# Expert blocks of 112 tokens instead of 128 in a mixture-of-experts layer on one core

## The reference, cut to what matters

```python
def moe_ffn(h, router_w, router_b, w_gu, b_gu, w_down, b_down):
    logits = _f32(xf @ router_w + router_b)
    top_v, top_i = lax.top_k(logits, TOP_K)          # TOP_K = 4 of N_EXPERTS = 32
    gates = jax.nn.softmax(top_v, axis=-1)
...
    def expert_block(args):
        x_blk, e = args
        gu = x_blk @ w_gu[e] + b_gu[e]               # (rows, 1024) @ (1024, 2048)
        gate = jnp.minimum(gu[:, :D_FF], SWIGLU_LIMIT)
        up = jnp.clip(gu[:, D_FF:], -SWIGLU_LIMIT, SWIGLU_LIMIT)
        act = (up + 1.0) * (gate * jax.nn.sigmoid(SWIGLU_ALPHA * gate))
        return act @ w_down[e] + b_down[e]           # (rows, 1024) @ (1024, 1024)
...
    y = jnp.zeros((N, D), h.dtype).at[stok].add(yb[dest] * sg[:, None].astype(h.dtype))
```

## Time and profile before

| | |
|---|---|
| time, median of 3 runs | 1618.28 us (1616.44 to 1618.72) |
| span of the profiled execution | 1615.2 us |
| TensorE busy | 1545.4 us, 96% of the span |
| VectorE busy | 1353.5 us, 84% |
| ScalarE busy | 988.6 us, 61% |
| GpSimd busy | 188.3 us, 12% |
| moved by DMA | 506.83 MB, 314 GB/s on average |

### The profile page before, as it was taken

How to read it: one execution, slowest core, us unless ns; L and a number is a source line. 1 busy time by engine, 2 the same in 40 slices (tenths; PEclk the granted TensorE clock), 3 DMA queues, 4 the chain that set the end, 5 groups by cost and what they waited for, 6 DMA issues and landing times.

```text
span 1615.2 us, 22190 instructions
## 1 busy us (share of the span) xinstructions
PE 1545.4 (96%) x8314; PEld 1169.8 (72%) x8314; DVE 1353.5 (84%) x1059; ACT 988.6 (61%) x798; POOL 188.3 (12%) x210
## 2 busy tenths in 40 slices
PE   3999989998999999999999999999999999999996
PEld 2444358857577787888888888888888888888873
DVE  5557447487878999999999999999999999999987
ACT  4112233343356776777777777777777777777772
POOL 1000111000101200000001000000110000010051
PEclk9999999998899999999999999999999999999998
DMA  9686121215569998999999999999999999999993
GB/s 374 251 342 235 43 92 29 67 57 205 215 251 351 358 384 334 389 387 387 382 387 375 382 396 386 384 389 384 384 378 387 389 385 389 381 390 376 374 380 121
DMA packets 85763, 506.83 MB, mean 314 GB/s; under 512 B 11008, under 2 KB 12336, under 8 KB 33360
## 3 DMA queue, kind: packets, MB, share of 16 engines
q1 hardware_dynamic: 70880, 453.85, 72.1%
q0 software_dynamic: 9104, 34.08, 5.8%
q10 hardware_dynamic: 5728, 18.18, 2.8%
HBM read 477.25 MB, written 28.84 MB: 313 GB/s over the span
## 4 chain that ended last, share of the span: by engine, by line
PE 85%; DVE 9%; DMA 2%; issue 1%; ACT 1%; SPq 0%; POOL 0%; DVEq 0%; POOLq 0%; ACTq 0%
PE ps L2132 62%; PE ps L1219 8%; PE ps L2148 2%; DVE w_lo L1481 2%; PE ps L1296 2%; PE ps L1225 2%; DMA Wt<-in_ada_w 2%; PE ps L2111 2%; PE ps L2121 1%; PE ps L2043 1%; PE ps L1194 1%; PE ps L1167 1%; DMA h_rows<-R 1%; PE ps L2154 1%; PE ps L1186 0%
## 5 line engine op out<-in xcount | busy, mean ns | idle before, releaser
L1481 DVE TENSOR_TENSOR w_lo<-w_raw,w_hi 128x2048 fp32r<-128x2048 f32 x384 | 865.0, 2288 | 72.9 <-ACT w_hi L1475 72.6
L1475 ACT ACTIVATE w_hi<-w_raw 128x2048 fp32r<-128x2048 f32 x384 | 736.6, 1920 | 293.1 <-PE ps L2132 293.1
L2132 PE MATMUL ps<-w_hi,xTh 128*128 128x512 f32 x1024 | 409.1, 399 | 6.5 <-DVE w_lo L1481 5.8
L2132 PE MATMUL ps<-w_lo,xTh 128*128 128x512 f32 x1024 | 402.4, 393 | 0.0
L2132 PE MATMUL ps<-w_hi,xTl 128*128 128x512 f32 x1024 | 276.1, 392 | 0.0
L2132 PEld LDWEIGHTS ps<-w_hi,xTh 128*128 128x128 f32 x1024 | 194.8, 190 | 60.5 <-issue 16.7
L2132 PEld LDWEIGHTS ps<-w_hi,xTl 128*128 128x128 f32 x1024 | 193.8, 189 | 40.6
L2132 PEld LDWEIGHTS ps<-w_lo,xTh 128*128 128x128 f32 x1024 | 194.7, 190 | 38.8
L2132 PE MATMUL ps<-w_hi,aTh 128*128 128x512 f32 x512 | 202.4, 395 | 0.0
L2132 PE MATMUL ps<-w_lo,aTh 128*128 128x512 f32 x512 | 199.4, 389 | 0.0
L2132 PE MATMUL ps<-w_hi,aTl 128*128 128x512 f32 x512 | 157.6, 389 | 0.0
(11 more groups left out here) (404 smaller groups left out, 1407.8 us busy)
## 6 DMA issues: line engine op xcount, KB each, us to landing
w_raw<-in_moe_w_gu SPq DMA_DIRECT2D x256, 1024.0 KB, 6.4
w_raw<-in_moe_w_down SPq DMA_DIRECT2D x128, 1024.0 KB, 7.2
Wt<-in_ada_w SPq DMA_DIRECT2D x19, 1024.0 KB, 10.3
y_rows<-R ACTq DMA_DIRECT2D x30, 512.0 KB, 6.7
Wt<-in_w_in SPq DMA_DIRECT2D x5, 2048.0 KB, 13.6
y_rows<-Wt POOLq DMA_DIRECT2D x1, 8704.0 KB, 40.5
R<-in_ada_w SPq DMA_DIRECT2D x5, 1024.0 KB, 8.1
R<-in_x SPq DMA_DIRECT2D x2, 2048.0 KB, 10.3
```

The source lines that it names most:

```text
L1475: nc.scalar.activation(w_hi[:, at[-1] % HI_SLOTS, :], w_raw[:, at[-1] % RAW_SLOTS, :], ACT.Copy).then_inc(hi_rdy, 1)
L1481: nc.vector.tensor_tensor(w_lo[:, s, :], w_raw[:, s, :], w_hi[:, at[-1] % HI_SLOTS, :].bitcast(F32), ALU.subtract).then_inc(lo_rdy, 1)
L2132: ins = mm(ps[:, bank0 + c, :], x[:, k, :], w[:, 512 * (banks * i + c):512 * (banks * i + c) + 512], start=(first and i == 0 and x is xh a ...
```

## The change

`BLK`, the tokens of a block, goes from 128 to 112. The overflow list has to grow, since more blocks could be needed in the worst case: `MAXOV` is now 2048 // 113 = 18 instead of 15, and `NB` 50 instead of 47. Everything that touches a block's tokens is cut to 112 columns or partitions. Division by 128 was a shift and becomes a sum of comparisons.

```diff
-BLK = 128
-MAXOV = 15
+BLK = 112
+MAXOV = TOPK * S // (BLK + 1)
 NB = E + MAXOV
...
-        slotI = sb("slotI", [P, TT * TOPK], U32)
-        ti = sb("ti", [P, TT * TOPK], U32)
...
-            pool.dma_start(y_d[(E - 2) * BLK:NB * BLK, :].rearrange("(b p) d -> p b d", p=P),
-                           zero_src.unsqueeze(1).to_broadcast([P, MAXOV + 2, D])).then_inc(y_zero, 16)
+            pool.dma_start(y_d[(E - 2) * BLK:NB * BLK, :].rearrange("(b p) d -> p b d", p=BLK),
+                           zero_src[0:BLK].unsqueeze(1).to_broadcast([BLK, MAXOV + 2, D])).then_inc(y_zero, 16)
...
-        xTh, xTl, aTh, aTl = [sb(name, [P, KT, BLK], F32R) for name in ("xTh", "xTl", "aTh", "aTl")]
+        xTh, xTl, aTh, aTl = [sb(name, [P, KT, P], F32R)[:, :, 0:BLK] for name in ("xTh", "xTl", "aTh", "aTl")]
...
-                nc.gpsimd.indirect_dma_start(out=xg[s], out_offset=None, in_=h2_d,
+                nc.gpsimd.indirect_dma_start(out=xg[s][0:BLK], out_offset=None, in_=h2_d,
...
-                s_.activation(dst[:], ps[:, 4:6, :].rearrange("p b (k t) -> p (b k) t", k=4), ACT.Copy
+                s_.activation(dst[:], ps[:, 4:6, :].rearrange("p b (k t) -> p (b k) t", k=4)[:, :, 0:BLK], ACT.Copy
...
-                act.dma_start(y_d[bass.ds(n * BLK, BLK), :], ysb[s]).then_inc(y_out[s], 16)
+                act.dma_start(y_d[bass.ds(n * BLK, BLK), :], ysb[s][0:BLK]).then_inc(y_out[s], 16)
...
-                link(v.tensor_copy(slotI[:, ks], slotf[:, ks]))
-                link(v.tensor_scalar(ti[:, ks], slotI[:, ks], 7, None, ALU.logical_shift_right))
-                link(v.tensor_copy(over[:, ks], ti[:, ks]))
+                link(v.tensor_scalar(over[:, ks], slotf[:, ks], float(BLK), None, ALU.is_ge))
+                for b in range(2, (S - 1) // BLK + 1):
+                    link(v.scalar_tensor_tensor(out=over[:, ks], in0=slotf[:, ks], scalar=float(BLK * b), in1=over[:, ks],
+                                                op0=ALU.is_ge, op1=ALU.add))
...
-            for b in range(2, S // BLK):
+            for b in range(2, (S - 1) // BLK + 1):
                 link(v.scalar_tensor_tensor(out=ovf[:], in0=total_e, scalar=float(BLK * b + 1), in1=ovf[:],
                                             op0=ALU.is_ge, op1=ALU.add))
...
-                v.tensor_tensor(lo_part[:], ps[:, 4:6, :].rearrange("p b (k t) -> p (b k) t", k=4),
+                v.tensor_tensor(lo_part[:], ps[:, 4:6, :].rearrange("p b (k t) -> p (b k) t", k=4)[:, :, 0:BLK],
                                 hi_part[:].bitcast(F32), ALU.subtract).then_inc(lo_sem, 1)
...
-                    ins = nc.tensor.transpose(ps[:, 4 + k // 4, P * (k % 4):P * (k % 4) + P],
-                                              xg[s][:, P * k:P * k + P], ident[:])
+                    ins = nc.tensor.transpose(ps[:, 4 + k // 4, P * (k % 4):P * (k % 4) + BLK],
+                                              xg[s][0:BLK, P * k:P * k + P], ident[0:BLK, 0:BLK])
...
-                        mm(ps[:, 2 * g + c, :], sel[rows, 0:1].to_broadcast([2 * E, P]), bparts[rows, g, :],
+                        mm(ps[0:BLK, 2 * g + c, :], sel[rows, 0:1].to_broadcast([2 * E, BLK]), bparts[rows, g, :],
...
-                                ins = mm(ps[:, bank0 + c, :], x[:, k, :],
+                                ins = mm(ps[0:BLK, bank0 + c, :], x[:, k, :],
```

More of the change, by code:

```diff
@@ L295, in build @@
         pick = Rc(19872, 19872 + TT * TOPK * E).rearrange("p (m e) -> p m e", e=E)
+        cmp = Rc(19872, 19872 + MAXOV * E).rearrange("p (m e) -> p m e", e=E)
         iotaL = Rc(14336, 14336 + BLK)
@@ L1545, in _ @@
             for s in range(2):
-                rows_of(tok[:, s:s + 1], s)
+                rows_of(tok[0:BLK, s:s + 1], s)
             with pool.Fori(1, E // 2) as m:
@@ L1876, in swiglu @@
                 wait_used(dve, gu_end)
-                v.tensor_scalar(two(act_b), ps[:, 2:4, :], 1.0 - LIMIT, 1.0 + LIMIT, ALU.max, ALU.min).then_inc(up_rdy, 1)
+                sig, act_ = sig_b[0:BLK], act_b[0:BLK]
+                v.tensor_scalar(two(act_), ps[0:BLK, 2:4, :], 1.0 - LIMIT, 1.0 + LIMIT, ALU.max, ALU.min).then_inc(up_rdy, 1)
                 dve.wait_ge(sig_rdy, n + 1)
                 dve.wait_ge(up_rdy, n + 1)
-                v.scalar_tensor_tensor(out=act_b, in0=sig_b, scalar=sat[:, 0:1], in1=act_b, op0=ALU.min,
+                v.scalar_tensor_tensor(out=act_, in0=sig, scalar=sat[0:BLK, 0:1], in1=act_, op0=ALU.min,
                                        op1=ALU.mult).then_inc(half_rdy, 1)
                 dve.wait_ge(half_rdy, n + 1)
-                v.scalar_tensor_tensor(out=two(act_b), in0=ps[:, 0:2, :], scalar=LIMIT, in1=two(act_b), op0=ALU.min,
+                v.scalar_tensor_tensor(out=two(act_), in0=ps[0:BLK, 0:2, :], scalar=LIMIT, in1=two(act_), op0=ALU.min,
                                        op1=ALU.mult).then_inc(act_rdy, 1)
@@ L2102, in _ @@
                 for block in ((block_p, block_t) if m >= TOPK else (block_p,)):
-                    ins = mm(ps[:, 6, 0:NB], lane_oh[:, m, :], block[:, m, :], start=(m == 0),
+                    ins = mm(ps[0:BLK, 6, 0:NB], lane_oh[:, m, :], block[:, m, :], start=(m == 0),
                              stop=(m == TT * TOPK - 1 and block is block_t))
@@ L2147, in at_turn @@
                     j, i = k // 2, k % 2
-                    ins = nc.tensor.transpose(ps[:, 4 + k // 4, P * (k % 4):P * (k % 4) + P],
-                                              act_b[:, 2 * P * j + i:2 * P * (j + 1):2], ident[:])
+                    ins = nc.tensor.transpose(ps[:, 4 + k // 4, P * (k % 4):P * (k % 4) + BLK],
+                                              act_b[0:BLK, 2 * P * j + i:2 * P * (j + 1):2], ident[0:BLK, 0:BLK])
                 ins.then_inc(at_mm, 1)
@@ L2188, in tail_turn @@
                     for t in range(TT):
-                        ins = nc.tensor.transpose(ps[:, 4 + i, P * t:P * t + P], tailG[:, TT * i + t, :], ident[:])
+                        ins = nc.tensor.transpose(ps[0:BLK, 4 + i, P * t:P * t + P], tailG[:, TT * i + t, :], ident[:])
                 ins.then_inc(tail_mm, 1)
```

27 lines of the change are left out of this document (13 added, 14 removed).

## The result

| | before | after |
|---|---|---|
| time, median of 6 runs each, side by side | 1617.26 us (1615.31 to 1618.72) | 1621.89 us (1620.71 to 1624.17) |
| span of the profiled execution | 1615.2 us | 1621.0 us |

The ratio is 1.003, 95% interval 1.0019 to 1.004: the change makes the kernel slower by 0.3%. The forecast was 1615.9 us with 1611.0 to 1620.7, so the time moved the other way and lies just outside the range. The two profiled spans differ by 5.9 us and the medians by 4.6: the rest is the spread from run to run.

The account below looks back on a forecast made before the run. The prediction took TensorE's matmul starts to bound the expert loop, with VectorE leading earlier from the routing on. Exposed loads -1.7, routing +0.4 and copies -1.1 gave -2.4 us from 1618.3: 1615.9 us, range 1611.0 to 1620.7.

Parts of the forecast that it names:

- The 4608 products: Experts' float32r matmuls on TensorE: fewer stationary columns leave their start distance unchanged; taken 0, bounds 0 and -2.3 us.
- Exposed loads: Four weight loads an expert that stand alone where the matmul stream breaks get an eighth shorter: -1.7 us.
- Transposes: 16 an expert on TensorE: the 128-column load sets their pace, so taken 0; -6.6 us if the stream did.
- Routing: VectorE's chain to the token list: extra comparison steps and changed one-hot sizes, +0.4 us in sum.
- The bf16 loads: 28 routing matmul loads, now 112 columns, keep their 25 ns pace: taken 0, other end +2.0 us.
- Rival 2: Products' 13.4 ns beyond their stream follow the loaded columns: 7.7 us more gain, 1608.2 us; chance 0.10.
- rival 1: Small bfloat16 routing loads lose their fast pace below 128 columns: +2.0 us, 1617.9 us; chance 0.33.
- Shorter copies: VectorE and ScalarE copies on the chain of waits, outside the TensorE-bound stretch, handle fewer elements: -1.1 us.
- rival 3: TensorE's clock falls once less (-2.8 us, chance 0.07) or once more (+2.8 us, chance 0.06) around the routing and early experts.
- Overflow: Overflow list stays empty, as the fullest expert has 96 tokens, below 112: nothing gained or lost.
- Rival 4: 4-byte loads under 128 columns take a slower way, exposed ones cost +13.3 us: 1630.9 us; chance 0.05.
- rival 5: Overflow list not empty: an entry costs a whole expert's weights, at least 35.4 us, over 1653 us; chance 0.02.

Follow-up runs that it names:

- e4: Kernel before with the experts' products and biases at 96 stationary columns instead of 128; products 230.0 ns apart, its time is not in the text.
- e6: Kernel before with the experts' products and biases at 80 stationary columns instead of 128; 1638 us.
- e8: e7 with blocks of 104 tokens instead of 112; 1615.79 us, ratio 0.9997 to the kernel before.
- e1: Kernel before with only the 4608 products at 112 stationary columns, biases and all else at 128; 1630.05 us, ratio 1.0061.
- e2: Kernel before with 32 bytes of unused memory ahead of the expert buffers, so only addresses move; 1617.9 us, ratio 1.0.
- e3: Kernel after with products, biases and the copies xTh, xTl, aTh, aTl back at 128 columns; 1615.07 us, ratio 0.9987 to the kernel before.
- e7: e3 with the lane one-hots of the bf16 routing matmuls also back at 128 columns; 1616.17 us, ratio 0.998 to the kernel before.
- e10: Kernel before with products and their biases at 112 stationary columns; 1630.73 us, ratio 1.0076.

## Why the prediction was wrong, step by step

- **The 4608 products, taken 0, bounds 0 and -2.3 us: this step failed.** Measured +2.27 ns x 4608 = +10.4 us. The mechanism was named only as what would make the prediction wrong ("a start distance of products that moves by a nanosecond"), and got no chance in the sum. Three things led there. First, the rows were of another kind of matmul. The earlier trace rows have 431 ns with 16 short loads among 48 and 429 without, and distance by distance the trace shows that these 2 ns are not in the short ones: the matmuls with 128 stationary columns start 429 ns apart, those with 8 start 429 ns apart, and a single break of 523 ns where the one follows the other makes the mean. The two halves of the row, first 128 columns, then 8:

```profile
160.72 13.04 PE L1219 MATMUL ps<-R,Wt 128*128 128x512 f32 x30
```

```profile
174.12 7.03 PE L1219 MATMUL ps<-R,Wt 128*8 128x512 f32 x16
```

(13.04 - 0.59)/29 and (7.03 - 0.59)/15 are both 0.429 us. So "120 columns less give 0" was read rightly for float32, which takes 429 ns for 512 columns; it did not carry over to float32r, which takes 227, and no row had a float32r product with fewer columns. Second, 0.32 - 0.094 is 0.226 and not 0.222 us, which leaves about 1 ns to the load and not 4: the lower bound of -2.3 us had no ground. Third, the upper bound was closed at 0 with no row behind it; nothing in the trace excluded a loss. Rival 2, with the sign of a gain, had 0.10, while the same size upward had no rival at all. The rule of the Trainium skill that was set aside (page "TensorE: Matmul & The Clock Gate", section "The mechanism" of Part 3: a load overlaps running matmuls only where the row groups differ) would have given a gain of 61 us, by the estimate of the prediction. The same section also has a load pulled ahead where it targets a background weight buffer, which the prediction left out. The traces disagree with the rule as the prediction used it, here even in sign: in e4 and e6, with a quarter and three eighths fewer columns to load, the products came later.
- **Exposed loads, -1.7 us: half right.** Behind the biases the second product follows the first after 327 ns instead of 338, behind the activations' transposes after 305 instead of 314, behind the gathered rows' after 300 instead of 314: 34 ns an expert, 1.1 us. The changes to and from the biases take 326 and 326 instead of 318 and 315, which gives 20 ns back, and the four biases by themselves, the fourth place counted, take 331 ns instead of 342. That leaves 26 ns an expert, 0.8 us.
- **Transposes, taken 0, bound -6.6 us: mis-sized.** The 8 of the gathered rows went from 109 to 96 ns, 7 distances or 0.090 us an expert, -2.8 us; those of the activations, with their stride of two, from 118.3 to 115.6 ns in the mean, -0.6 us, and the product behind them follows after 55 ns instead of 39, which takes 0.5 back. The router's matmuls were the wrong neighbours: they come at 0.11 us with 32 moving columns, but the transposes, with as many columns to load, came down to 96 and in e8 to 89 ns, so the load does not set a transpose's pace at 109 ns (the transposes' loads also last 140 ns in the trace, the router's 190).
- **Routing, +0.4 us: right.** From the first operation of `lanes` to the first list load 13.08 us before (396.71 to 409.79) and 13.48 after (398.40 to 411.88). The rows, as the earlier trace rows:

```profile
398.40 0.56 DVE L1762 TENSOR_TENSOR R<-R,ps 128x384 f32<-128x384 f32 x1 [0.51 <-PE ps L2068]
...
399.79 0.58 DVE L1768 SCALAR_TENSOR_TENSOR R<-R 128x12 f32<-128x12 f32 x3
...
400.70 1.55 DVE L1774 TENSOR_TENSOR R<-R 128x1344 bf16<-128x1344 f32 x1
...
410.01 0.99 DVE L1846 TENSOR_TENSOR R<-R 128x800 bf16<-128x800 f32 x1
```

- **The bf16 loads, taken 0, other end +2.0: rival 1 was the right mechanism**, at 52 ns and not 98: +0.75 us. The "nearest row" was the same instruction at full width, which could not tell.
- **Shorter copies, -1.1 us: right for each piece** (`aTl` 1.14 to 1.00 us; `xTl` 1.13 to 1.00; the eight L1948 2.05 to 1.99 us, less than thought). For expert 0 the gain of `xTh` did not reach the product: it was ready at 420.54 us, and VectorE came to `xTl` at 420.89, behind two pieces of `w_lo`. The gather, taken 0 and at best -0.6, gave the 0.48 us above. The chain after:

```profile
518.68 1.00 DVE aTl L1888
...
601.32 1.99 DVE R L1948 x8
...
607.10 1.00 DVE xTl L1888
```

- **The clock, rival 3.** It moved, and it explains why 2.34 us at the first product became 0.35 at expert 1. Granted clock (the column before the last two) in two stretches, before and then after (0.5 would be 1.2 GHz, 1.00 is 2.4):

```profile
390.00:410.00 20.00, 15.09 (x66) 9.49 (x66) 17.36 (x59) 9.85 (x8) 0.00 (x0) 0.66 0.80 322
410.00:425.00 15.00, 12.31 (x65) 7.85 (x62) 13.18 (x18) 3.54 (x8) 4.10 (x6) 0.77 0.30 106
```

```profile
390.00:410.00 20.00, 17.04 (x66) 11.70 (x67) 16.09 (x55) 11.12 (x10) 0.00 (x0) 0.57 0.88 358
410.00:425.00 15.00, 11.49 (x69) 6.86 (x68) 13.84 (x24) 3.47 (x7) 4.69 (x6) 1.00 0.28 91
```

Before, the clock fell to 1.2 GHz between 417.4 and 424.2 us, under the first products of expert 0 (72 in 18.72 us); after, it did not (72 in 16.75 us), but it was low for longer just before. The falls are no effect of the change that was shown, and they move from run to run: in e1, whose program is that of before up to its products, the clock is low from 391.4 to 408.5 and from 418.7 to 422.1 us. Of the 1.69 us of delay ahead of `lanes`, 0.16 stand at 232 us and 1.64 from 246 us on: between them the clock was low for 6.8 us instead of 3.4, before anything had changed on the way but the zero fill. The 72 products at full clock give 1.97 us back, and so the delay vanishes with the one fall less. The slow loop does not.
- **Overflow, DMA, moved buffers at 128 columns: right at 0**, as far as the runs tell: TensorE ran 8314 matmuls before and after, so no overflow block was computed; TensorE waited for no DMA in the loop; and e2 has the ratio 1.0, within 0.2%. Rival 4 had a slower load way as its mechanism; the loads show none (174 ns after 188), and the loss came while loads were hidden.

By the measured terms, over 31 steps: products +9.7 (138 distances an expert), breaks and biases -0.8, transposes of the gathered rows -2.8, those of the activations -0.6 and the product behind them +0.5, which makes +6.0 in the loop, as the period has it (31 x 0.193 = +6.0); around it +0.4, +0.75, -0.5 for the gather and about -1 for the copies, and +1.7 and -2.0 with the clock. That makes 5.4 of the 5.9 us between the two profiled spans; the rest was not followed up. Two sums of the prediction besides: rival 5's "over 1653 us" starts from the 1618.3 before and not from the forecast, which would give 1651; and with the transposes' term set right the forecast would have been about 3 us lower, so that it is in part luck that it lies only 6 us off.

## What to carry to other kernels

A matmul whose load is hidden does not get cheaper with fewer stationary columns, and can get dearer: the float32r products here did (by 1 to 6 ns of 227), the float32 matmuls did not (429 ns with 128 and with 8). In this kernel, where a block takes fewer rows, the better choice was to cut the moving side (transposes, copies) and leave the stationary operand at its full 128 columns, as in e3 and e7, for 0.1 to 0.2%. When thousands of equal instructions set the time, a nanosecond of start distance is a term of its own with a sign of its own: bound it on both sides, from a row of the same data type, and where a row's mean is off by 2 ns, look at its distances one by one before reading a rule into it.

## What was not expected of the hardware

- Products of 512 float32r columns start 226.7 ns apart with 128 stationary columns, and later at each smaller width that was run: 227.8 at 124, 228.9 or 233.3 at 112, 230.0 at 96, 233.1 at 80, though the load gets shorter (188 to 148 ns). Why is open. Float32 matmuls of 512 columns start 429 ns apart with 128 and with 8 stationary columns alike.
- At 112 columns there are two stable patterns of distances, 4.4 ns apart in the mean, the same in every expert of a run; 32 bytes of moved buffers switched one stretch in the kernel after (6 us), and none in e10 or at 128 columns. What picks the pattern is open.
- bf16 loads of 112 columns come every 52 ns, of 128 columns every 25.
